# Rotary embedding of q and k: the half turn by VectorE's shuffle within 32 partitions in place of a product with a permutation matrix

## The chip, the cores and the metric

One Trainium2 chip, one of its cores. The metric is the time of one execution of the whole program on the device, in microseconds (us). A core has TensorE (matrix products into PSUM), VectorE, ScalarE (called ACT), GpSimd (called POOL) and SyncE (SP), which here only starts DMAs. The engines run their own instruction lists and meet through semaphores.

## What is computed

One inference step of a two-layer backbone for 128 context tokens and 512 latent tokens, D_MODEL 1024. Each layer: an input projection, windowed attention beside a long convolution, gates, an output projection, a layer norm, a gated MLP with a short convolution, and a second layer norm. The part that matters here is the rotary embedding of q (8 heads of 64) and k (2 heads), on the latent tokens only:

```python
def axial_rope(x):
    ...
    ang = jnp.stack([ang, ang], axis=-2).reshape(L, HEAD_DIM)
    cos = jnp.cos(ang)[None, :, None, :]
    sin = jnp.sin(ang)[None, :, None, :]
    xf = x.astype(jnp.float32)
    xa = xf.reshape(x.shape[:-1] + (2, 2, HEAD_DIM // 4))
    rot = jnp.stack([-xa[..., 1, :], xa[..., 0, :]], axis=-2).reshape(x.shape)
    return (xf * cos + rot * sin).astype(x.dtype)
...
q, k, v, z_hy, gate_a, gate_b = jnp.split(h @ lp['w_in'], SPLITS, axis=-1)
...
attn = latent_attention(axial_rope(q), axial_rope(k), v, ctx_k, ctx_v, lp['attn_sink'])
```

Within each 32 features, `rot` swaps the two halves of 16 and negates the one that comes first.

## The kernel before

**Layout.** Activations lie with features on the 128 partitions and tokens in the free dimension: q is four rows of 128 features (two heads each), k one row, v one row, each of 644 columns, of which 512 are latent (`LAT`) and 128 context (`CTX`). Swapping 16 features with their neighbours is therefore a move between partitions.

**Weights.** A weight chunk comes from HBM into one of two `w_raw` buffers (SP, line 518). ACT rounds it to its high part (`split` at line 1121, `w_hi`), VectorE subtracts that from the raw one to get the low part (`split` at line 1641, `w_lo`), and TensorE makes three products per block, high by high, low by high and high by low (`tile`, line 636 inside; `opening`, line 689, for q). Chunks 0 and 1 are q, 2 is k, 3 is v, 4 to 9 are z, two tiles each. VectorE's `split(n)` raises `w_split`, on which both TensorE and the load of a later chunk wait.

**The order by hand.** Every engine's list is written out. For the start of a layer:
- TensorE (lines 871 to 900): q, k, v; then `rotated(0)` to `rotated(3)`; z's first tile (`tile(4, 0, ...)`); `rotated(4)`; transposes of v, of the cached keys and of k's context part; z's second tile; then the scores of block 0 (`qk`), which wait for `rot_out` 5, that is for all five ropes.
- VectorE (lines 1871 to 1887): `split(2)`, `split(3)`, `split(4)`; the waits for the sine and cosine rows (`trig_in`) and, in layer 0, for earlier stores (`g_spill`); four ropes; `split(5)`; the fifth rope; `soft(0)`.
- ACT (lines 1266 to 1305): copies of q's halves out of PSUM, high parts of the chunks, copies of k and v (`qkv_out` counts them), and the copies of the transposes (`vt_out`).
- POOL (line 2208) loads `trig` once a layer, clears pad columns, and later stores the context keys and values.

`ROPE_ORDER` is k first, then q's rows 0 to 3. A rope (line 1696) waits for its product in PSUM, multiplies its row by the cosine, the product by the sine into a scratch (`tmp`, in the space of `scores`), and adds the two. The product is taken by `rotated` with the 128x128 matrix `rot`, which is loaded at the start of the program among the constants (line 1051, ACT's queue).

Of the kernel before, what the change touches and what calls it, by code (L numbers as in the profile page):

```python
# [24 lines left out]
ALU = mybir.AluOpType  # L25

P = 128
# [90 lines left out]
for _name, _n in (("b_ada", 48), ("hy_w", 36), ("hy_b", 12), ("hy_bias", 4), ("ln1_g", 8),  # L118
# [22 lines left out]
    qkv_mm=10, qkv_out=10, rot_mm=5, rot_out=5, vt_mm=2, vt_out=4,  # L141
# [93 lines left out]
def _program(nc, A):  # L235
# [11 lines left out]
    def sb(name, shape, dt=F32, where=st):  # L247
        return where.enter_context(nc.sbuf_tensor(name, shape, dt))
# [7 lines left out]
    rot = sb("rot", [P, P])  # L256
# [126 lines left out]
    ROPE_ORDER = [4, 0, 1, 2, 3]  # L383
# [143 lines left out]
    def _(pe):  # L527
# [92 lines left out]
        pe.wait_ge(sem["consts_in"], 16 * 3)  # L620
# [234 lines left out]
        for L in range(DEPTH):  # L855
# [19 lines left out]
            def rotated(at):  # L875

                r = ROPE_ORDER[at]
                pe.wait_ge(sem["qkv_out"], due("qkv_out", 5 + r))
                src = q[:, r, LAT] if r < 4 else k[:, 0, LAT]
                mm(ax[:, at % 4, :], rot[:, :], src, start=True, stop=True).then_inc(sem["rot_mm"], raised("rot_mm"))  # L880

            for at in range(4):
                rotated(at)
            pe.wait_ge(sem["w_split"], due("w_split", splits(4)))
            tile(4, 0, KD, 0, h_mov, "z_mm")
            pe.wait_ge(sem["rot_out"], due("rot_out", 1))
            rotated(4)
            pe.wait_ge(sem["qkv_out"], due("qkv_out", 10))
            pe.wait_ge(sem["rot_out"], due("rot_out", 3))
# [151 lines left out]
    def _(act):  # L1041
# [8 lines left out]
        for dst, src in ((mask_in, "mask"), (rot, "rot"), (ones, "ones")):  # L1050
            act.dma_start(dst[:, :], A[src]).then_inc(sem["consts_in"], 16)
# [445 lines left out]
    def _(dve):  # L1497
# [198 lines left out]
        def rope(r):  # L1696
# [4 lines left out]
            dve.wait_ge(sem["rot_mm"], due("rot_mm", at + 1))  # L1701
            dve.wait_ge(sem["qkv_out"], due("qkv_out", 5 + r))
            TT(row, row, trig[:, 0, :], ALU.mult).then_inc(sem["dve_order"], raised("dve_order"))
            TT(tmp, ax[:, at % 4, :], trig[:, 1, :], ALU.mult).then_inc(sem["dve_order"], raised("dve_order"))
# [150 lines left out]
        for L in range(DEPTH):  # L1855
# [15 lines left out]
            for g in range(1, 4):  # L1871
                split(g + 1)
# [3 lines left out]
            for r in ROPE_ORDER[:4]:  # L1876
                rope(r)
# [247 lines left out]
    def _(pool):  # L2125
# [61 lines left out]
        for L in range(DEPTH):  # L2187
            lane.start(L)
            if L == 0:
                pool.dma_start(par[:, 0:NPAR], A["par"][L]).then_inc(sem["params_in"], 16)  # L2190
                pool.wait_ge(sem["consts_in"], 16 * 3)
# [150 lines left out]
def _shape_constants():  # L2342
# [5 lines left out]
    r = np.zeros((P, P), np.float32)  # L2348
    for a in range(0, P, 32):
        for i in range(16):  # L2350
            r[a + 16 + i, a + i] = -1.0
            r[a + i, a + 16 + i] = 1.0
    out["rot"] = r
# [4 lines left out]
    out["trig"] = np.ascontiguousarray(np.stack([np.cos(ang), np.sin(ang)], axis=1).astype(np.float32))  # L2358
# [113 lines left out]
```

## Time and profile before

| | |
|---|---|
| median of 3 runs | 2025.42 us (2023.16 to 2025.57) |
| span of the profiled execution | 2021.7 us |
| instructions | 30180 |
| TensorE matmul busy | 1963.4 us, 97% |
| TensorE weight load busy | 1881.6 us, 93% |
| VectorE busy | 1166.7 us, 58% |
| ACT busy | 746.1 us, 37% |
| POOL busy | 199.1 us, 10% |

The profile is one execution. A row of the timeline begins with its start from the beginning of the span and its duration; in brackets stands how long the engine had been idle before it and what ended that. Matmuls overlap one another, so the sum of their durations is more than the time that they take. The chain of waits is followed back from the last instruction, at each step to what released it or to the instruction before it on its engine. Layer 0 of the network begins near 80 us, layer 1 near 1060 us; the rotation of layer 0 lies between 137 and 151 us, that of layer 1 between 1095 and 1109 us.

### The profile page before, as it was taken

How to read it: one execution, taken by the hardware profiler on the slowest of the kernel's cores; microseconds unless marked ns; L12 is line 12 of the kernel's file. 1: busy time of each engine (PE TensorE's matmuls, PEld its weight loads, DVE VectorE, ACT ScalarE, POOL GpSimd, SP SyncE). 2: the span in 40 equal slices, each digit the busy share in tenths (PEclk: the TensorE clock that was granted, in tenths of full speed). 3: DMA queues.
4: the chain of work that ended last, by engine and by line, in shares of the span. 5: the costliest groups of instructions: out<-in, count | busy, mean ns of one | idle time of the engine just before them, and what ended most of it. 6: DMA issues, size and time to landing. Idle time of an engine off the chain costs nothing.

```text
span 2021.7 us, 30180 instructions
## 1 busy us (share of the span) xinstructions
PE 1963.4 (97%) x12914; PEld 1881.6 (93%) x12914; DVE 1166.7 (58%) x1739; ACT 746.1 (37%) x1102; POOL 199.1 (10%) x218
## 2 busy tenths in 40 slices
PE   8899998999999999999999999899999999999996
PEld 3599998999999999999989999899998999999996
DVE  7735658787476777767454556852346343333335
ACT  3634445322273321333244445532227332133313
POOL 0211001100150000000121101110015000000011
PEclk9999999999999999999999999899999999999999
DMA  8522013255213345343322211322212221221121
GB/s 333 194 83 99 19 58 129 101 203 173 82 63 145 127 153 198 142 164 129 104 75 97 84 37 57 111 76 76 94 64 71 77 71 58 91 84 63 64 72 53
DMA packets 38911, 211.00 MB, mean 104 GB/s; under 512 B 4487, under 2 KB 8120, under 8 KB 20217
## 3 DMA queue, kind: packets, MB, share of 16 engines
q1 hardware_dynamic: 31480, 184.78, 25.6%
q0 software_dynamic: 4208, 17.55, 2.4%
q10 hardware_dynamic: 3088, 6.75, 0.9%
q8 instruction: 101, 1.65, 0.3%
q14 instruction: 34, 0.27, 0.0%
HBM read 198.82 MB, written 10.24 MB: 103 GB/s over the span
## 4 chain that ended last, share of the span: by engine, by line
PE 84%; DVE 9%; ACT 4%; issue 3%; POOL 0%; ACTq 0%; DMA 0%; SPq 0%; DVEq 0%; POOLq 0%
PE gemm_psum L636 51%; PE gemm_psum L666 15%; PE gemm_psum L689 3%; PE gemm_psum L649 3%; PE aux_psum L776 2%; PE gemm_psum L709 2%; PE aux_psum L757 2%; PE aux_psum L765 1%; ACT h_src_rows L1211 1%; PE gemm_psum L543 1%; PE gemm_psum L581 1%; DVE aux_psum L1820 1%; PE aux_psum L799 1%; DVE x L1824 1%; DVE w_lo L1654 0%
## 5 line engine op out<-in xcount | busy, mean ns | idle before, releaser
L636 PE MATMUL gemm_psum<-h_hi,w_hi 128*128 128x322 f32 x2144 | 497.1, 313 | 0.2
L636 PE MATMUL gemm_psum<-h_hi,w_lo 128*128 128x322 f32 x2144 | 493.4, 311 | 0.0
L636 PE MATMUL gemm_psum<-h_lo,w_hi 128*128 128x322 f32 x2144 | 491.5, 310 | 0.0
L636 PEld LDWEIGHTS gemm_psum<-h_hi,w_hi 128*128 128x128 f32 x2144 | 362.7, 189 | 4.4 <-issue 3.1
L636 PEld LDWEIGHTS gemm_psum<-h_lo,w_hi 128*128 128x128 f32 x2144 | 362.2, 189 | 0.0
L636 PEld LDWEIGHTS gemm_psum<-h_hi,w_lo 128*128 128x128 f32 x2144 | 362.0, 189 | 0.0
L1645 DVE TENSOR_TENSOR w_lo<-w_raw,w_hi 128x2048 fp32r<-128x2048 f32 (+4 forms) x124 | 237.1, 1912 | 180.1 <-ACT w_hi L1134 179.1
L1134 ACT ACTIVATE w_hi<-w_raw 128x2048 fp32r<-128x2048 f32 (+4 forms) x128 | 204.1, 1595 | 170.7 <-PE gemm_psum L666 65.6
L1552 DVE CUSTOM_DVE_ANT_0 aux_psum<-w_raw,cond_by_row 128x1024 f32<-128x1024 f32 x160 | 191.0, 1257 | 4.5 <-DMA w_raw<-in_ada_t 4.1
L1778 DVE SCALAR_TENSOR_TENSOR x<-gemm_psum,mod,x 128x128 f32<-128x128 f32 (+2 forms) x144 | 55.4, 434 | 160.6 <-PE gemm_psum L666 130.8
L666 PE MATMUL gemm_psum<-act_hi,w_lo 128*128 128x322 f32 x616 | 142.0, 312 | 0.0
L666 PE MATMUL gemm_psum<-act_lo,w_hi 128*128 128x322 f32 x616 | 141.6, 311 | 0.0
L666 PE MATMUL gemm_psum<-act_hi,w_hi 128*128 128x322 f32 x616 | 141.5, 311 | 0.0
L1680 DVE SCALAR_TENSOR_TENSOR gate_acc<-gate_rows,par,gate_acc 128x642 f32<-128x642 f32 x88 | 80.2, 912 | 76.1 <-ACT gate_acc L1219 74.6
L1851 DVE TENSOR_TENSOR gate_acc<-gate_acc,gemm_psum 128x644 f32<-128x644 f32 x40 | 33.0, 826 | 143.7 <-PE gemm_psum L636 143.7
L666 PEld LDWEIGHTS gemm_psum<-act_hi,w_hi 128*128 128x128 f32 x616 | 104.2, 189 | 0.0
L666 PEld LDWEIGHTS gemm_psum<-act_hi,w_lo 128*128 128x128 f32 x616 | 104.2, 189 | 0.0
L666 PEld LDWEIGHTS gemm_psum<-act_lo,w_hi 128*128 128x128 f32 x616 | 104.0, 189 | 0.0
L1160 ACT ACTIVATE act_hi<-gate_acc 128x644 fp32r<-128x644 f32 x44 | 32.7, 742 | 153.5 <-DVE gate_acc L1851 147.1
L1218 ACT ACTIVATE gate_rows<-gemm_psum 128x644 f32<-128x644 f32 (+1 forms) x48 | 31.8, 663 | 143.7 <-PE gemm_psum L636 139.3
L2184 POOL TENSOR_TENSOR sums<-x 128x644 f32<-128x644 f32 x4 | 6.3, 1579 | 790.5 <-DVE x L1778 790.5
L689 PE MATMUL gemm_psum<-h_hi,w_hi 128*128 128x322 f32 x224 | 72.2, 322 | 10.3 <-DVE w_lo L1654 3.4
(352 smaller groups left out, 3279.7 us busy)
## 6 DMA issues: line engine op xcount, KB each, us to landing
w_raw<-in_w_up SPq DMA_DIRECT2D x44, 1024.0 KB, 4.8
w_raw<-in_ada_t SPq DMA_DIRECT2D x42, 1024.0 KB, 4.7
w_raw<-in_w_down SPq DMA_DIRECT2D x32, 704.0 KB, 4.1
w_raw<-in_w_gate SPq DMA_DIRECT2D x16, 1024.0 KB, 4.7
w_raw<-in_w_z SPq DMA_DIRECT2D x12, 1024.0 KB, 4.7
w_raw<-in_w_out SPq DMA_DIRECT2D x8, 1024.0 KB, 4.7
g_kept<-g_rows_out POOLq DMA_DIRECT2D x10, 512.0 KB, 3.0
ada_early<-in_ada SPq DMA_DIRECT2D x4, 1024.0 KB, 19.5
```

The costliest lines, as they stand in the source:

```text
L636: last = mm(gp[:, 2 * (t % 2) + hf, 0:HALF], w[:, off + P * kk:off + P * (kk + 1)], moving(kk, lo)[:, hf * HALF:(hf + 1) * HALF], start=kk ...
L649: last = mm(gp[:, 2 * (t % 2) + hf, 0:HALF], w[:, off + P * kk:off + P * (kk + 1)], moving(kk, lo)[:, half(hf)], start=kk == 0 and n == 0, ...
L666: last = mm(gp[:, 2 * (t % 2) + hf, 0:HALF], w[:, off + P * kk:off + P * (kk + 1)], moving(kk, lo)[:, half(hf)], start=kk == 0 and n == 0, ...
L689: last = mm(banks(c, p_, hf), w[:, P * (KD * c + kk):P * (KD * c + kk + 1)], (hlo if lo else hhi)[:, kk, half(hf)], start=kk == 0 and n == ...
L709: last = mm(gp[:, 2 * ((t0 + c) % 2) + hf, 0:HALF], w[:, P * (KD * c + kk):P * (KD * c + kk + 1)], moving(kk, lo)[:, hf * HALF:(hf + 1) * ...
L757: last = mm(ax[:, n % 4, at:at + P * m], q[pr, j, tok(b)], rhs, start=True, stop=True)
L776: last = mm(ax[:, 2, HD * n:HD * (n + 1)], p_t(n)[:, P * kb:P * (kb + 1)], v[:, HD * (n % 2):HD * (n % 2 + 1)], start=kb == 0, stop=kb == ...
L1134: run(whi[s][:, 0:n], raw[st_ % 2][:, 0:n], ACT.Copy).then_inc(sem["w_hi"], raised("w_hi"))
L1552: V.tensor_tensor_reduce(out=ada_out[:, :] if first else ax[:, 2 * gr:2 * gr + 2, :].rearrange("p a b -> p (a b)"), in0=raw[n % 2][:, D_MO ...
L1645: TT(wlo[s][:, 0:n], raw[STEP[(lane.layer, "g", g)] % 2][:, 0:n], f32(whi[s][:, 0:n]), ALU.subtract).then_inc(sem["w_split"], raised("w_sp ...
L1680: STT(acc[:, 1:ROW - 1], z[:, a:a + ROW - 2], w(tap), acc[:, 1:ROW - 1], ALU.mult, ALU.add).then_inc(sem[event if tap else "dve_order"], r ...
L1778: STT(x[:, m, a:b], gp[:, 2 * (t % 2) + h, a - HALF * h:b - HALF * h], mod[:, gate + m, gr:gr + 1], x[:, m, a:b], ALU.mult, ALU.add)\
```

## The change

The matrix `rot`, its load, the five products of a layer and the semaphore `rot_mm` are removed. A rope begins with a `stream_shuffle` of its row into `tmp`, with the list `HALF_TURN`, the same for each group of 32 partitions; the multiply with the cosine waits for it, since it overwrites the row. The sign is moved into the sine rows, which are made on the host. The ropes' order is now q's rows 0 to 3, then k; on VectorE two ropes stand ahead of `split(4)` and two behind it, and k's rope stands behind `split(5)`. TensorE's waits for single ropes ahead of `rotated(4)` and the transposes are gone; the one for all five ahead of the scores stays. The waits for the constants count two loads instead of three.

```diff
-    qkv_mm=10, qkv_out=10, rot_mm=5, rot_out=5, vt_mm=2, vt_out=4,
+    qkv_mm=10, qkv_out=10, rot_out=5, vt_mm=2, vt_out=4,
...
-    rot = sb("rot", [P, P])
...
-    ROPE_ORDER = [4, 0, 1, 2, 3]
+    ROPE_ORDER = [0, 1, 2, 3, 4]
+    HALF_TURN = [(i + 16) % 32 for i in range(32)]
...
-        pe.wait_ge(sem["consts_in"], 16 * 3)
+        pe.wait_ge(sem["consts_in"], 16 * 2)
...
-            def rotated(at):
-
-                r = ROPE_ORDER[at]
-                pe.wait_ge(sem["qkv_out"], due("qkv_out", 5 + r))
-                src = q[:, r, LAT] if r < 4 else k[:, 0, LAT]
-                mm(ax[:, at % 4, :], rot[:, :], src, start=True, stop=True).then_inc(sem["rot_mm"], raised("rot_mm"))
-
-            for at in range(4):
-                rotated(at)
             pe.wait_ge(sem["w_split"], due("w_split", splits(4)))
             tile(4, 0, KD, 0, h_mov, "z_mm")
-            pe.wait_ge(sem["rot_out"], due("rot_out", 1))
-            rotated(4)
             pe.wait_ge(sem["qkv_out"], due("qkv_out", 10))
-            pe.wait_ge(sem["rot_out"], due("rot_out", 3))
...
-        for dst, src in ((mask_in, "mask"), (rot, "rot"), (ones, "ones")):
+        for dst, src in ((mask_in, "mask"), (ones, "ones")):
...
-            dve.wait_ge(sem["rot_mm"], due("rot_mm", at + 1))
             dve.wait_ge(sem["qkv_out"], due("qkv_out", 5 + r))
+            V.stream_shuffle(tmp, row, HALF_TURN).then_inc(sem["dve_order"], raised("dve_order"))
+            dve.wait_ge(sem["dve_order"], now("dve_order"))
             TT(row, row, trig[:, 0, :], ALU.mult).then_inc(sem["dve_order"], raised("dve_order"))
-            TT(tmp, ax[:, at % 4, :], trig[:, 1, :], ALU.mult).then_inc(sem["dve_order"], raised("dve_order"))
+            TT(tmp, tmp, trig[:, 1, :], ALU.mult).then_inc(sem["dve_order"], raised("dve_order"))
...
-            for g in range(1, 4):
+            for g in range(1, 3):
                 split(g + 1)
...
-            for r in ROPE_ORDER[:4]:
+            for r in ROPE_ORDER[:2]:
+                rope(r)
+            split(4)
+            for r in ROPE_ORDER[2:4]:
                 rope(r)
...
-                pool.wait_ge(sem["consts_in"], 16 * 3)
+                pool.wait_ge(sem["consts_in"], 16 * 2)
...
-    out["trig"] = np.ascontiguousarray(np.stack([np.cos(ang), np.sin(ang)], axis=1).astype(np.float32))
+    sign = np.where(np.arange(P) % 32 < 16, -1.0, 1.0)[:, None]
+    out["trig"] = np.ascontiguousarray(np.stack([np.cos(ang), sign * np.sin(ang)], axis=1).astype(np.float32))
```

## Rows read from the trace of the kernel before

**Rows 1.** The page, parts 1 and 4: busy time, and the last chain.
```profile
PE 1963.4 (97%) x12914; PEld 1881.6 (93%) x12914; DVE 1166.7 (58%) x1739; ACT 746.1 (37%) x1102; POOL 199.1 (10%) x218
...
PE 84%; DVE 9%; ACT 4%; issue 3%; POOL 0%; ACTq 0%; DMA 0%; SPq 0%; DVEq 0%; POOLq 0%
```

**Rows 2.** TensorE's waits: for whom, us in total, times, longest.
```profile
PE aux_psum L837 <- DVE y_lo L1658: 13.9, 2, 7.0
```

**Rows 3.** Windows: stretch, length; busy PE, PEld, DVE, ACT, POOL; clock, DMA share, GB/s.
```profile
137.00:158.00 21.00, 20.95 (x128) 18.11 (x126) 11.96 (x17) 5.64 (x10) 1.61 (x3) 1.00 0.38 132
```

**Rows 4.** The tile `rot`: durations in ns (min/median/max), first and last start.
```profile
L880 PE MATMUL aux_psum<-q,rot x16: 590/591/593, 138.7 to 1106.8; 128*128 128x512 f32 x16
```

**Rows 5.** Timeline of TensorE's weight loads, 137 to 142 us.
```profile
137.64 0.34 PEld L880 LDWEIGHTS aux_psum<-k,rot 128*128 128x128 f32 x2
138.22 0.19 PEld L880 LDWEIGHTS aux_psum<-q,rot 128*128 128x128 f32 x1 [0.24 <-issue]
...
140.80 0.19 PEld L636 LDWEIGHTS gemm_psum<-h_hi,w_hi 128*128 128x128 f32 x1 [0.24 <-issue]
...
141.38 0.34 PEld L636 LDWEIGHTS gemm_psum<-h_lo,w_hi 128*128 128x128 f32 x2
```

**Rows 6.** The chain of waits in order of time: start, duration, what.
```profile
137.95 3.44 PE aux_psum L880 x8
...
148.54 0.86 PE aux_psum L880 x2
...
157.31 0.47 PE aux_psum L757 x4
...
1106.54 0.86 PE aux_psum L880 x2
```

**Rows 7.** Timeline of VectorE at the start of each layer.
```profile
124.85 1.23 DVE L1645 TENSOR_TENSOR w_lo<-w_raw,w_hi 128x1024 fp32r<-128x1024 f32 x1 [5.91 <-ACT w_hi L1134]
132.85 2.29 DVE L1645 TENSOR_TENSOR w_lo<-w_raw,w_hi 128x2048 fp32r<-128x2048 f32 x1 [6.78 <-ACT w_hi L1134]
139.02 0.69 DVE L1703 TENSOR_TENSOR k<-k,trig 128x512 f32<-128x512 f32 x1 [3.88 <-PE aux_psum L880]
139.63 0.68 DVE L1704 TENSOR_TENSOR scores<-aux_psum,trig 128x512 f32<-128x512 f32 x1
140.34 0.69 DVE L1706 TENSOR_TENSOR k<-k,scores 128x512 f32<-128x512 f32 x1
140.95 0.69 DVE L1703 TENSOR_TENSOR q<-q,trig 128x512 f32<-128x512 f32 x1
...
1090.85 2.29 DVE L1645 TENSOR_TENSOR w_lo<-w_raw,w_hi 128x2048 fp32r<-128x2048 f32 x1 [6.78 <-ACT w_hi L1134]
```

**Rows 8.** VectorE by line and form (busy, mean ns), and one row of its timeline.
```profile
L1820 DVE RECIPROCAL aux_psum<-aux_psum 128x322 f32<-128x322 f32 x8 | 17.3, 2168 | 0.0
...
8.00 0.43 DVE L1515 TENSOR_SCALAR sine_turns<-h1T 128x512 f32<-128x512 f32 x1
```

**Rows 9.** Timeline of ACT, 124 to 140 us.
```profile
124.72 0.42 ACT L1239 ACTIVATE q<-gemm_psum 128x322 f32<-128x322 f32 x1
130.90 1.92 ACT L1134 ACTIVATE w_hi<-w_raw 128x2048 fp32r<-128x2048 f32 x1 [5.76 <-PE gemm_psum L636]
...
138.59 1.90 ACT L1134 ACTIVATE w_hi<-w_raw 128x2048 fp32r<-128x2048 f32 x1
```

**Rows 10.** Timeline of POOL, 95 to 108 us.
```profile
95.77 0.57 POOL L2161 DMA_DIRECT2D g_kept<-g_rows_out  x1 [0.16 <-issue]
...
107.25 0.57 POOL L2208 DMA_DIRECT2D trig<-in_trig  x1 [0.30 <-POOL h_lo L2152]
```

**Rows 11.** The start: ACT's queue, and a wait of TensorE's weight loads.
```profile
7.63 0.52 ACTq L1051 DMA_DIRECT2D rot<-in_rot  x1
...
PEld gemm_psum L543 <- DMA ada_early<-in_ada: 0.8, 1, 0.8
```

**Rows 12.** Windows behind the long convolution's wait in each layer, columns as in rows 3.
```profile
345.00:360.00 15.00, 13.75 (x89) 12.52 (x87) 14.00 (x28) 13.11 (x22) 7.85 (x6) 1.00 0.10 42
...
1300.00:1315.00 15.00, 14.51 (x96) 13.82 (x96) 13.42 (x27) 13.03 (x22) 5.68 (x6) 0.94 0.20 71
```

More of the change, by code:

```diff
@@ L2346, in _shape_constants @@
     out["ones"] = np.ones((P, P), np.float32)
[L2348 to L2353, printed above, removed]
     inv = 1.0 / (10000.0 ** (np.arange(0, 32, 2, dtype=np.float32) / np.float32(32)))
```

## The prediction

> **What bounds the kernel now.** I read the page first: TensorE is busy for 97% of the span, and the chain that ended last is 84% TensorE work [rows 1]. A microsecond taken out of TensorE's own stream is therefore worth a microsecond, unless the place where it is taken out is one where TensorE waits. The waits of TensorE come next: the longest in the whole kernel is 7.0 us, twice, once a layer, on `y_lo` of the long convolution [rows 2], and no wait there names the rotation. Then the stretch from 137 to 158 us, which holds the rotation of layer 0: TensorE is busy in 20.95 of 21.00 us, VectorE in 11.96, the granted clock is 1.00 (its 2.4 GHz level) [rows 3]. So this stretch is TensorE's, and VectorE has room in it.
>
> **Removed: the products with the permutation matrix.** A product is two passes. The tile view lists 16 passes for q's 8 products, 591 ns each [rows 4], and 4 more for k's 2. But passes overlap, so 591 ns is not the price. The price is the distance between weight loads: 137.64, 138.22, ..., and 141.38 where the z product is back at its own pace, in rows 0.43 us apart (138.22 to 140.80 holds six of them, 2.58 us) [rows 5]. The chain of waits says the same: 3.44 us for the 8 passes ahead of z's tile and 0.86 us for the two in the middle of it, 0.86 us again in layer 1 [rows 6]. That is 10 passes x 0.43 = 4.30 us a layer, 8.60 us in both, all of it on TensorE's stream with no wait inside. The neighbours (the v, z and transpose work) keep their lengths.
>
> **Added: a shuffle in each rope, on VectorE.** Before, a rope is three operations of 128x512; its rhythm is 139.02 to 140.95, 1.93 us. An operation that waits for the one in front starts 0.71 us behind it (139.63 to 140.34) [rows 7]. The change puts one more operation in front, and the multiply with the cosine, which overwrites the row, waits for it. No shuffle is in the trace. From below I bound it by a single-source operation of this size, 0.43 us; from above by the slowest kind per column that VectorE has here, the reciprocal, 2.168 us for 322 columns, so by proportion 3.45 us for 512 [rows 8]. I take the ordinary two-source operation, 0.69 us, a slot of 0.71, because it moves the same bytes: a rope is then 2.64 us.
>
> The Trainium skill (VectorE: DVE Perf Modes, "The perf-mode tier table") gives a shuffle no faster mode, about 2400 ns for 2048 columns beside 2293 for a two-source one; by that a 512-column shuffle would be an estimated 0.80 us, and the rope 2.75 us. The Trainium skill (Vector Engine (DVE) Microarchitecture Reference, 3.8 The reshape front-end and per-opcode configuration) also says that an instruction of its own loads the lane selection first, so there may be two new instructions to a rope, not one. Neither would move the sum, for the cover below is far wider; no row here shows either.
>
> **What covers the ropes, and what is late next.** Order on VectorE before: the low parts of k, v and z (`split(2)` to `split(4)`), ropes k, q0, q1, q2, `split(5)`, rope q3. After: `split(2)`, `split(3)`, ropes q0, q1, `split(4)`, ropes q2, q3, `split(5)`, rope k. Before, VectorE is idle for 6.78 us in front of `split(4)` and for 3.88 us in front of the first rope [rows 7]. What moves in front of `split(4)` must be ready by 126.08, the end of `split(3)` (124.85 + 1.23): the last of q's four rows is copied at 124.72 + 0.42 [rows 9], the sine and cosine rows are asked for at 107.25, and the last spill that the ropes of layer 0 wait for is issued at 95.77 [rows 10]. So ropes q0 and q1 run from 126.08 to 131.36. `split(4)` needs ACT's high part, done at 130.90 + 1.92 = 132.82 [rows 9], so it starts at 132.85 and ends at 135.14 as before, with 1.5 us to spare. TensorE wants it at 137.64 [rows 5], 2.5 us later still. The same places in layer 1 stand at 1090.85, again behind 6.78 us of idle time [rows 7].
>
> Behind it, q2 and q3 run to 140.42; ACT's high part for `split(5)` is done at 138.59 + 1.90 = 140.49 [rows 9], hung on the v product's end and so unmoved; `split(5)` ends at about 142.8 and rope k at 145.5. TensorE reaches the scores of block 0, which wait for all ropes, at 157.31 before [rows 6] and at 153.01 after. Rope k, now the last, has 7.5 us of cover. The cost of the added VectorE work (5 x 0.71 = 3.6 us a layer) is therefore nothing. If the first cover is gone, each further microsecond of a rope delays `split(4)` by two; the place and point are priced below. Nobody is queued behind the moved `split(4)` but the load of the next weights, whose issue is tied to it: at the old time. `split(5)` finishes at 142.8 instead of 149.03 (139.02 + 4 x 1.93 + 2.29), so the load behind it goes out 6 us sooner; it lands ahead of need either way, so I cost it at nothing. The wait of the transposes on the ropes (`rot_out` 3) goes too; it was over before they were reached, and v's row, which they do need, was copied long before.
>
> **Everything behind.** ACT's copies of v, GpSimd's stores and combines, and the scores all hang on TensorE's transposes and tiles, which move together by 4.30 us, so they keep their places to one another. In the long convolution TensorE's 7.0 us wait hangs on a VectorE chain which itself starts from a product of TensorE, so it moves along.
>
> **At the start** the load of `rot` leaves ACT's queue: 0.52 us of issuing ahead of the first sine [rows 11]. Gain at most 0.55 us. I take 0: TensorE soon waits 0.8 us for the landing of the first modulation weights [rows 11], more than the half microsecond. From the other side, the loads behind it start that much sooner and share the engines with those weights, so a loss of as much is possible.
>
> **Clock.** Behind the 7.0 us waits the granted clock sinks below its upper level; 15 us on it is 1.00 in layer 0 but 0.94 in layer 1 [rows 12], that is 15 x 0.06 = 0.9 us that one layer pays and the other does not, at otherwise equal work. A shift of 4.3 us can flip this in either layer: 0 taken, -0.9 to +1.8 as bounds.
>
> **The sum** is made against the profiled execution, 2021.7 us of span, 3.7 us below the median 2025.42 of the runs shown (lowest 2023.16): 2021.7 - 8.60 = 2013.1 us of span, and by the same 3.7 us a median of 2016.8 us, 0.42% less.
>
> **Rivals.**
> - *A slow shuffle, the side on which it loses.* With a rope of r us, `split(4)` is late by 2r - 9.27 (from 126.08 to 137.64, less 2.29 for the split), and from its end the scores by 3r + 2.29 - 15.06 more (three ropes and `split(5)` against z's tiles and the transposes: 157.31 - 141.39 - 0.86 = 15.06 by [rows 6]). Together 5r - 22.04; it eats the 4.30 us at r = 5.27, a shuffle slot of 3.34 us, and loses 0.2% only from a slot of 3.74 us. At the reciprocal's pace, slot 3.47 and r 5.40, each layer loses 0.66 us: 2026.7 us. For it: that no row shows a shuffle, and that its lanes cross. Against: a reciprocal computes and a shuffle only moves, as the operation of 0.43 us does, and the rope's own three take 0.69 us [rows 7, 8]. Chance 0.04, with half of that beyond 0.2% slower.
> - *The gain stops at the long convolution.* If the VectorE chain behind the 7.0 us wait had its foot off TensorE, the wait would grow to 11.3 us and the time stay at 2025.4; in one layer only, 2021.1. Against: the chain of waits runs through TensorE's transposes and z tiles up to that stage. Chance 0.06 for both layers, 0.06 for one.
> - *The passes were hidden.* Were part of the 4.30 us hidden by something that z's product waits for anyway, the time would lie between. Against: the weight loads follow without a stop at both ends [rows 5]. With a give-back of 2 to 4 us by the clock or the loads it makes 2019 to 2021: chance 0.04.
>
> **How the numbers follow.** The forecast, a gain of 8.6 us with its small terms, has 0.80. Its own range: -0.55 and -0.9 below, +0.5 and +1.8 above, and below that the runs of before, which reach 2.3 us under their median: 2013.8 to 2019.5. To keep no more than 2 in 10 outside, the upper end takes in part of the one-layer case: 2013.5 to 2020.5. About 0.2% (4.05 us) is what a measurement of this kernel can tell from no change. Faster by more than that, under 2021.4, are the forecast, the one-layer case and the partly hidden passes: 0.90. Within it: the case of both layers and half the slow shuffle, 0.08. Slower: 0.02.
>
> **What would show it.** In the profile after: no passes of the rotation; the v product followed at once by z's first tile, near 137.6; five shuffles a layer of some 0.7 us; two ropes ended ahead of `split(4)`, which still starts by 133; no wait of TensorE that names the low part of z or rope k; the scores of block 0 near 153; the wait on `y_lo` still 7 us. A shuffle slot over 1.45 us would shift `split(4)`, one over 2.70 us would stop TensorE. A longer `y_lo` wait, or a clock in the convolution stage below that of before, would make the number wrong.

## The result, and the profile after

| | before | after |
|---|---|---|
| median | 2025.22 us (2023.16 to 2025.57, 4 runs) | 2034.55 us (2031.60 to 2035.25, 4 runs) |
| span of the profiled execution | 2021.7 us | 2033.4 us |

After divided by before is 1.0045, 95% interval 1.0032 to 1.0058: slower, where 2016.8 us and faster were predicted. (The two profiled executions are 11.7 us apart, the medians 9.3 us: before's profile is near the fastest of its executions, after's is the slowest.) The instruction counts moved by what the diff says: 20 TensorE passes fewer and 20 VectorE instructions more than in [rows 1] (ten shuffles, each with a small instruction ahead of it). Page of the profile after, parts 1, 3 and 4; q10 is ACT's DMA queue:

```profile
PE 1957.1 (96%) x12894; PEld 1879.5 (92%) x12894; DVE 1172.7 (58%) x1759; ACT 745.6 (37%) x1102; POOL 199.2 (10%) x218
...
q10 hardware_dynamic: 2944, 6.69, 0.9%
...
PE 82%; DVE 9%; ACT 4%; issue 2%; ACTq 1%; DMA 1%; POOL 0%; SPq 0%; DVEq 0%
```

What is new in it is "ACTq 1%": 1% of a chain of 2033 us, where [rows 1] has 0%, spent in issuing a DMA. TensorE's waits in the profile after (for whom, us in total, times, longest) say where:

```profile
PE aux_psum L553 <- ACT h1T L1081: 19.1, 1, 19.1
PE aux_psum L837 <- DVE y_lo L1646: 13.9, 2, 7.0
```

The second line is [rows 2], unmoved. The first is the first use of ACT's sines, at the very start of the program; before, the same wait was 2.7 us long:

```profile
PE aux_psum L553 <- ACT h1T L1093: 2.7, 1, 2.7
```

ACT's timeline after, and under it the same stretch of before:

```profile
8.26 0.62 ACTq L1040 DMA_DIRECT2D x<-in_x_prompt  x1
8.91 17.57 ACTq L1041 DMA_DIRECT2D x<-in_x_sample  x1
26.51 1.28 ACT L1043 ACT_TABLE_LOAD   x1 [26.51 <-issue]
```

```profile
8.73 0.62 ACTq L1052 DMA_DIRECT2D x<-in_x_prompt  x1
9.38 0.76 ACTq L1053 DMA_DIRECT2D x<-in_x_sample  x1
10.17 1.28 ACT L1055 ACT_TABLE_LOAD   x1 [10.17 <-issue]
```

The issue of the last load of the start, x_sample, takes 17.57 us instead of 0.76. Nobody wants x before 78 us (in before), but ACT's list stands still behind it, and its first sine comes 16.3 us later. So the loss is at the start, far from the rotation. The rotation itself did what was predicted. The chain of waits after, in both layers (start, duration, what; L636 is the product of v and then of z, L757 the scores of block 0):

```profile
140.48 21.44 PE gemm_psum L636 x144
...
169.83 0.47 PE aux_psum L757 x4
...
1097.09 21.45 PE gemm_psum L636 x144
...
1126.44 0.47 PE aux_psum L757 x4
```

v's product begins at 140.48 where before it began at 123.66 (16.82 us later), but the scores begin at 169.83 against 157.31 [rows 6], only 12.52 us later: 4.30 us won between them, as predicted. In layer 1 it is 1097.09 against 1081.66 (15.43 later) and 1126.44 against 1115.31 (11.13 later): 4.30 us again. Between the two rotations this execution lost 2.91 us (12.52 to 15.43), and 0.57 us behind the second (11.13 to the 11.7 of the whole span). 2.0 of the 2.9 us went ahead of layer 0's output product, which begins at 520.58 against 506.06. VectorE's timeline after, which answers to [rows 7]:

```profile
142.82 0.01 DVE L1690 LOAD_MASK_SELECT scores<-q  x1
142.82 0.73 DVE L1690 STREAM_SHUFFLE scores<-q 128x512 f32<-128x512 f32 x1
143.58 0.69 DVE L1692 TENSOR_TENSOR q<-q,trig 128x512 f32<-128x512 f32 x1
...
145.53 0.01 DVE L1690 LOAD_MASK_SELECT scores<-q  x1
...
149.68 2.29 DVE L1633 TENSOR_TENSOR w_lo<-w_raw,w_hi 128x2048 fp32r<-128x2048 f32 x1 [1.35 <-ACT w_hi L1122]
```

A shuffle takes 0.73 us, its slot is 0.76 us (142.82 to 143.58), a rope 2.71 us (to 145.53). `split(4)` still waits 1.35 us for ACT: the two ropes ahead of it are covered.

### The profile page after: what moved, and what is told of

Read it like the earlier page. It is cut to its first block, busy times and chain, and to the rows that moved or that the text cites. A ratio compares the mean times of both kernels' runs of the same rounds, so it can differ in the third digit from the quotient of the medians.

```text
span 2033.4 us, 30146 instructions
## 1 busy us (share of the span) xinstructions
PE 1957.1 (96%) x12894; PEld 1879.5 (92%) x12894; DVE 1172.7 (58%) x1759; ACT 745.6 (37%) x1102; POOL 199.2 (10%) x218
## 3 DMA queue, kind: packets, MB, share of 16 engines
q10 hardware_dynamic: 2944, 6.69, 0.9%
## 4 chain that ended last, share of the span: by engine, by line
PE 82%; DVE 9%; ACT 4%; issue 2%; ACTq 1%; DMA 1%; POOL 0%; SPq 0%; DVEq 0%
PE gemm_psum L636 49%; PE gemm_psum L666 15%; PE gemm_psum L689 3%; PE gemm_psum L649 3%; PE aux_psum L776 2%; PE gemm_psum L709 2%; PE aux_psum L757 2%; PE aux_psum L799 1%; PE aux_psum L765 1%; ACT h_src_rows L1199 1%; PE gemm_psum L581 1%; ACTq L1041 1%; DVE aux_psum L1809 1%; DVE w_lo L1642 1%; PE gemm_psum L543 1%
## 5 line engine op out<-in xcount | busy, mean ns | idle before, releaser
L636 PE MATMUL gemm_psum<-h_hi,w_hi 128*128 128x322 f32 x2144 | 496.6, 313 | 1.8 <-DVE w_lo L1642 1.2
L636 PE MATMUL gemm_psum<-h_hi,w_lo 128*128 128x322 f32 x2144 | 493.5, 311 | 0.0
L636 PE MATMUL gemm_psum<-h_lo,w_hi 128*128 128x322 f32 x2144 | 491.5, 310 | 0.0
L636 PEld LDWEIGHTS gemm_psum<-h_hi,w_hi 128*128 128x128 f32 x2144 | 362.5, 189 | 5.7 <-issue 2.8
L636 PEld LDWEIGHTS gemm_psum<-h_lo,w_hi 128*128 128x128 f32 x2144 | 362.2, 189 | 0.0
L636 PEld LDWEIGHTS gemm_psum<-h_hi,w_lo 128*128 128x128 f32 x2144 | 362.0, 189 | 0.0
L689 PE MATMUL gemm_psum<-h_hi,w_hi 128*128 128x322 f32 x224 | 72.3, 323 | 10.7 <-POOL h_lo L2144 3.7
## 6 DMA issues: line engine op xcount, KB each, us to landing
ada_early<-in_ada SPq DMA_DIRECT2D x4, 1024.0 KB, 19.5
```

The costliest lines, as they stand in the source:

```text
L636: last = mm(gp[:, 2 * (t % 2) + hf, 0:HALF], w[:, off + P * kk:off + P * (kk + 1)], moving(kk, lo)[:, hf * HALF:(hf + 1) * HALF], start=kk ...
L689: last = mm(banks(c, p_, hf), w[:, P * (KD * c + kk):P * (KD * c + kk + 1)], (hlo if lo else hhi)[:, kk, half(hf)], start=kk == 0 and n == ...
```

## The experiments

### Is it the missing load?

The theory with which I began: ACT's queue had room for x_sample only because of what stood ahead of it. The rivals were the shuffle and everything else in the diff. Two runs, one that puts a load back and one that makes only that part of the change.

**e1_load_back**: after, with a load of 64 KB in the place of the one of `rot`, into a tile that nobody reads.

```diff
-        for dst, src in ((mask_in, "mask"), (ones, "ones")):
+        for dst, src in ((mask_in, "mask"), (spare, "ones"), (ones, "ones")):
```

> The changed kernel with a 64 KB load put back on ACT's queue where the matrix was loaded, into a tile that nobody reads; its source is the matrix of ones, so the matrix of the permutation stays away from the program. Theory A (the start is lost because ACT's queue has one load less, everything else of the prediction holds): the issue of x_sample falls from 17.57 us back to about 0.8 us, the median is that of before less 8.6 us, 2016.6 us. Rival B (the loss comes from the addresses or the set of tensors, not from the queue): 2034 us as the changed kernel. Rival C (the shuffles cost elsewhere too): between, over 2020 us.

Measured: 2018.25 us median (2017.36 to 2019.15, 5 runs) against 2025.41 for before, ratio 0.9964 (0.9950 to 0.9978), span 2016.4. The stop is gone, by one unread load (ACT's timeline):

```profile
9.39 0.77 ACTq L1042 DMA_DIRECT2D x<-in_x_sample  x1
```

**e2_before_rot_on_pool**: before, with only the load of `rot` moved from ACT's queue to POOL's.

```diff
-        for dst, src in ((mask_in, "mask"), (rot, "rot"), (ones, "ones")):
+        for dst, src in ((mask_in, "mask"), (ones, "ones")):
...
+                pool.dma_start(rot[:, :], A["rot"]).then_inc(sem["rot_in"], 16)
```

> The kernel before, products and all, with one part of the change alone: the matrix is no longer loaded on ACT's queue but on POOL's. Theory A: ACT's issue of x_sample stalls for some 17 us and the time is 2025 + 17 = 2042 us, with no shuffle in the program. Rival B (tensors or addresses): no stall, 2025 us.

Measured: 2042.42 us, span 2040.2, with all the products of the rotation in it. ACT's timeline:

```profile
8.86 17.62 ACTq L1054 DMA_DIRECT2D x<-in_x_sample  x1
```

The stop is there without a shuffle and without any other part of the change, and costs what it costs in after. So the load that left ACT's queue is the cause; the two runs show it from both sides. They also settle rival B: e2 keeps the tensor `rot` and its tile where they were, and still stops.

### What in the load matters?

Its 64 KB, its moment (half a microsecond), its number in the list, or its packets? A packet here is one piece of a load on one DMA engine. The page's part 3 gives the measure: ACT's queue has 3088 packets before and 2944 after, that is 193 and 184 for each of the 16 DMA engines. The load of `rot` is the difference, 9 packets on each; a load of x is 65. Ahead of x_sample stand 128 on each engine before (seven loads of 9 and x_prompt) and 119 after. The Trainium skill (DMA: Bandwidth & Descriptors, "Queues, rings and completion order") says that each queue has a ring of its own on each DMA engine, with its own tail pointer, which is why I count by engine; it gives no size at which an issue stops.

**e3_one_packet**: after, with a load of 16 partitions in the place of `rot` (2 packets on each engine where `rot` had 9, so 121 ahead; "a ninth" in the expectation is wrong).

```diff
+        act.dma_start(spare[0:16, :], A["ones"][0:16, :]).then_inc(sem["consts_in"], 16)
```

> As the run that puts a load back, but of 16 partitions of 512 bytes, 8 KB: nearly the same time of issuing, a ninth of the packets. If what counts is when x_sample is issued (8.91 us in the changed kernel, 9.38 us before) or how many loads stand ahead of it, no stall: 2016.6 us. If what counts is how many packets stand ahead of it in the queue, the stall is there: 2034 us.

**e4_wait**: after, ACT issues x_sample only when two sines' arguments are there, 2 us later.

```diff
+        act.wait_ge(sem["mlp_arg"], 2)
         act.dma_start(x[:, :, LAT], A["x_sample"]).then_inc(sem["x_in"], 16)
```

> The changed kernel; ACT waits for VectorE's second piece of sine arguments (near 10.9 us) before it issues x_sample. If the moment of the issue decides, the stall is gone and the time 2017 to 2019 us; if the packets ahead of it decide, the issue still ends near 26.5 us and the time is 2034 us.

**f2_swapped**: after, x_sample ahead of x_prompt.

> The changed kernel with x_sample issued ahead of x_prompt. Theory D (the large load of 2 MB is what can't be taken): x_sample, now with fewer packets ahead, stalls. Theory E: x_sample goes from 54 to 119 and is issued in 0.8 us, x_prompt goes from 119 to 184 and stalls to about 26.5 us; time 2034 us.

**f4_in_halves**: after, x_sample in two loads of four rows each.

```diff
+        act.dma_start(x[:, 0:4, LAT], A["x_sample"][:, 0:4]).then_inc(sem["x_in"], 16)
+        act.dma_start(x[:, 4:8, LAT], A["x_sample"][:, 4:8]).then_inc(sem["x_in"], 16)
```

> The changed kernel with x_sample loaded in two halves of 33 packets per DMA engine. Theory E: the first half (119 to 152) passes 128 and stalls; if the stall lasts until what is behind 128 has room, its issue ends earlier than 26.5 us (a shorter piece behind the mark), and the second half then takes the rest of the wait; time 2030 to 2034 us. Theory D (one load must not be larger than some size): no stall, 2017 us.

Measured, all four with the loss still there: 2034.94, 2034.70, 2036.04 and 2035.03 us. ACT's timelines, e3, e4, f2 and f4 in this order:

```profile
9.40 18.09 ACTq L1043 DMA_DIRECT2D x<-in_x_sample  x1
```

```profile
11.08 15.32 ACTq L1042 DMA_DIRECT2D x<-in_x_sample  x1
```

```profile
8.28 0.62 ACTq L1040 DMA_DIRECT2D x<-in_x_sample  x1
8.93 17.56 ACTq L1041 DMA_DIRECT2D x<-in_x_prompt  x1
```

```profile
8.80 17.61 ACTq L1041 DMA_DIRECT2D x<-in_x_sample  x1
26.44 0.53 ACTq L1042 DMA_DIRECT2D x<-in_x_sample  x1
```

e3: a load in the old place, but of 2 packets in place of 9, does not help. x_sample is asked for at 9.40, as before the change, and behind as many loads, so neither the count of loads nor half a microsecond decides. e4: 2.2 us later, the stop ends at the same 26.40 us. f2: the other load stops when it stands second, so it is the place and not the tensor. f4: half a load stops as long as a whole one (not for a shorter time, as theory E had it), and the half behind it does not stop at all. The load that stops has 119 (or 121) packets ahead of it, whatever it is.

### The rule: first theory wrong

By then I held that ACT stops on the load whose packets pass the 128th, since before the change x_prompt ended exactly at 128. Two runs on either side of it.

**g2_one_packet_less**: as e1, but the load put back has 112 partitions (8 packets on each engine; x_sample has 127 ahead).

> The kernel after with the load put back as in the run that removed the stall, but of 112 partitions instead of 128: one packet less on each DMA engine of ACT's queue (8 instead of 9), so x_prompt ends at the 127th and x_sample goes from the 128th to the 192nd. Theory 'position': x_sample passes the 128th, so it stops for 15 to 18 us and the span is 2031 to 2036 us. Rival 'any load in that place of about this size is enough': no stall, 2015 to 2019 us of span.

**g1_two_loads**: after with two loads of 9 packets more (x_prompt has 72 ahead and passes 128, x_sample has 137). The second one is 112 columns wide, 56 KB; f1, the same with two full tiles, has no time, since SBUF was 64 bytes a partition short for it.

> The kernel after with two 64 KB loads ahead of the two loads of x (one of them in the place of the load of rot, the other behind that of ones), so that ACT's queue holds 72 packets of each DMA engine ahead of x_prompt instead of 63 (before) or 54 (after). Theory 'position': ACT stops on the load whose packets pass the 128th of each engine of its queue; now x_prompt does that (72 to 137), so x_prompt's issue takes 15 to 18 us and x_sample's under 1 us, and the span is 2031 to 2036 us. Rival 'enough ahead': the stall comes only when too little stands ahead of x_sample; then neither stops, and the span is 2015 to 2019 us. If x_sample stops again and x_prompt doesn't, both are wrong.

Measured: g2 2032.89 us, as the theory has it; g1 2039.69 us, but not as it has it. ACT's timelines, g2 and then g1:

```profile
9.32 18.18 ACTq L1043 DMA_DIRECT2D x<-in_x_sample  x1
```

```profile
9.19 0.62 ACTq L1043 DMA_DIRECT2D x<-in_x_prompt  x1
9.84 17.79 ACTq L1044 DMA_DIRECT2D x<-in_x_sample  x1
```

In g1 x_prompt passes the 128th and takes 0.62 us; x_sample stops with 137 ahead. So passing 128 is not it. What is left is that it goes by how much stands ahead, with 128 as an exception. One packet less (g2) or nine more (g1) than before the change, and the stop is there.

**g4_other_128**: after, nothing added, mask and ones in two pieces each and x_prompt in eight: 128 ahead of x_sample, in 16 loads.

```diff
+            for a in (0, 64):
+                act.dma_start(dst[a:a + 64, :], A[src][a:a + 64, :]).then_inc(sem["consts_in"], 16)
+        for j in range(8):
+            act.dma_start(x[:, j, CTX], A["x_prompt"][:, j]).then_inc(sem["x_in"], 16)
```

> The kernel after with the loads ahead of x_sample cut up, nothing added: mask and ones in two pieces of 64 partitions each, x_prompt in eight (one for each row of 128 features). A piece costs one more packet on each DMA engine, so 36 + 4 x 5 + 8 x 9 = 128 packets of each engine stand ahead of x_sample, as before the change, but in 16 loads instead of 8. Theory 'exactly 128': x_sample's issue takes under 1 us (the start is later by the 9 more issues, 0.5 us each, so the span is 2018 to 2023 us). Rival 'it is not the count: the stall comes in any list other than the one of before (seven constants and one load of x)': x_sample or one of the pieces ahead of it takes 10 to 18 us, and the span is over 2028 us.

**g5_fewer_ahead**: after, ones behind the loads of x: 110 ahead of x_sample, 175 ahead of ones.

> The kernel after with the load of ones moved behind the two loads of x: 45 packets of each DMA engine ahead of x_prompt and 110 ahead of x_sample (after: 54 and 119). Theory A: whoever is issued with more than some number between 72 and 110 ahead stops, unless that number is 128; then x_sample's issue takes 14 to 18 us, ending near 26 us, and the span is over 2030 us. Theory B: the bound lies between 110 and 119 (as it would if only a load passing 175 to 184 in total stopped); then x_sample takes under 1 us and ones, with 175 ahead, stops in its place. In either case the time itself says little, since ones lands behind x.

Measured: 2038.11 and 2035.77 us. ACT's timelines, g4 (three narrow stretches show pieces alone) and g5:

```profile
11.83 4.53 ACTq L1042 DMA_DIRECT2D x<-in_x_prompt  x1
11.83 8.66 ACTq L1042 DMA_DIRECT2D x<-in_x_prompt  x2
...
20.51 6.08 ACTq L1042 DMA_DIRECT2D x<-in_x_prompt  x2
26.62 0.61 ACTq L1043 DMA_DIRECT2D x<-in_x_sample  x1
```

```profile
8.42 15.27 ACTq L1040 DMA_DIRECT2D x<-in_x_sample  x1
23.73 6.27 ACTq L1041 DMA_DIRECT2D ones<-in_ones  x1
```

In g4 the first four pieces (56, 65, 74 and 83 ahead) go out at 0.45 to 0.63 us each; the fifth, with 92 ahead, ends at 16.36, the sixth (101) at 20.49, the seventh (110) at 23.54, the eighth (119) at 26.59. And with 110 ahead g5's x_sample, a load seven times as large, ends at 23.69: theory A of its expectation, though ones, with 175 ahead, stops as well. Beside each other, with what is left of the packets ahead at that moment (counted as below):

| packets ahead on each engine | runs | the issue ends at (us) | left on each engine |
|---|---|---|---|
| 54 to 83 | all that ask for one at the start | at once | |
| 92, 101 | g4 | 16.36, 20.49 | 72, 75 |
| 110 | g4, g5 | 23.54, 23.69 | 76 |
| 119 | after, e2, e4, f2, f4, g4, g6 | 26.40 to 26.59 | 78 to 79 |
| 121, 127, 137 | e3, g2, g1 | 27.49, 27.50, 27.63 | 77, 83, 92 |
| 128 | before, e1, e5, h1 | at once (0.76 to 0.78 us) | 122 |
| 128 | g4 | at once (asked at 26.62) | 88 |
| 152 | f4 | at once (asked at 26.44) | 111 |
| 175 | g5 | 30.00 | 111 |

How far the queue is by then can be counted. The DMA view of the profile after from 0 to 26.5 us (packets, MB, share of the engines' time):

```profile
q10 hardware_dynamic: 661, 3.89, 35.4%
```

661 / 16 = 41 of the 119 are through, so 78 stand in the queue when the issue goes on; over the rows from 92 to 121 it is 72 to 79. It fits that g4's piece with 83 ahead was asked for with some 73 left and did not stop, and the next one, with 92 ahead, was asked for with some 81 left (181 packets through) and did. That explains why the stop is so long: it lasts until some 40 packets of each engine, most of them of 4 to 12 KB, have gone through engines that carry the modulation weights at the same time.

What is shown is that the issue of a load stops its engine until the queue has drained some way, and that up to 121 ahead it goes on with 72 to 79 left. One bound for all rows is not shown: with 127, 137 and 175 ahead the stop ended with 83, 92 and 111 left, f4's second half went at once with 111 left and g4's x_sample with 88. The exception of 128 rests on four kernels with one and the same list (seven loads of 9 packets and one of 65); g4 could not decide between "exactly 128" and "that list", since its own 128 was reached only when the queue had drained. Both stay open.

### Can the loads go elsewhere?

**f3_x_later**: after, both loads of x issued by ACT behind the first rows of the filter spectrum (34 us); no load put back.

> The changed kernel with both loads of x issued by ACT behind its first two copies of the filter spectra (near 33 us), when its queue has drained, and no load put back. The stall is gone: the gain of 8.6 us stands alone, 2016.6 us, or up to 1 us less since ACT issues 2 us less ahead of its first sine (TensorE waits there for the first modulation weights anyway). If x then lands late for layer 0 (needed near 79 us) or ACT's issues push the filter work, 2018 to 2020 us.

**g6_x_in_gap**: the same at 24 us, ahead of a stretch in which ACT is idle.

```diff
         pre_split(1)
+        act.dma_start(x[:, :, CTX], A["x_prompt"]).then_inc(sem["x_in"], 16)
+        act.dma_start(x[:, :, LAT], A["x_sample"]).then_inc(sem["x_in"], 16)
```

> The kernel after with both loads of x issued by ACT behind the high part of the second filter block (near 25 us, in a stretch where ACT is idle for 3.48 us) instead of ahead of the first sine; no load put back. Theory: the stall needs over 72 packets of each engine outstanding, and by then the constants are nearly through, so none of the two stops; the issues (1.4 us) fall into idle time, the first sine comes 1.4 to 2.0 us earlier than in the run with the load put back, and TensorE's wait of 2.7 us for it shrinks. Span 2013.5 to 2016.5 us, median 2015 to 2018.5 us. Rival: the earlier sine only brings TensorE to a wait for the modulation weights, which land when they land: no gain over the run with the load put back (span 2016 to 2017). If x_sample stalls at the new place, the span is over 2018 us.

**g3_x_on_pool**: after, both issued by POOL.

> The kernel after with both loads of x issued by POOL (behind its load of par), which waits until 31 us for the constants anyway; no load put back. ACT's queue then holds 54 packets of each DMA engine at the start and never passes 128 there. Theory 'position': ACT does not stop; its first sine comes 1.4 us earlier than in the run with the load put back (8.8 instead of 10.2 us), and the two loads are POOL's, where the second may stop behind 128 of its own (65 + 65 and par's 9) at no cost if it ends before 31 us. Span 2014 to 2018 us, median 2016 to 2020 us. Rival 'the shuffle or the lost load slows the start in another way': a wait of TensorE of over 10 us ahead of 31 us stays, and the span is over 2030 us. Contrary possibility: POOL stops for longer than until 31 us and delays the mask and the first low parts; then the span lies between 2018 and 2032 us.

**e5_load_back_again**: e1's kernel beside g6.

> The same kernel as the run with the load put back, for comparison with the one ahead of it on the same chip: median 2016.5 to 2019.5 us, span 2015.5 to 2017.5 us, x_sample's issue 0.8 us.

| | median (runs) | before | ratio (95%) | span |
|---|---|---|---|---|
| f3_x_later | 2018.64 (6) | 2025.09 | 0.9967 (0.9955 to 0.9979) | 2018.1 |
| g6_x_in_gap | 2018.84 (6) | 2024.96 | 0.9970 (0.9958 to 0.9981) | 2017.9 |
| g3_x_on_pool | 2025.45 (10) | 2025.30 | 1.0001 (0.9991 to 1.0010) | 2025.4 |
| e5_load_back_again | 2016.88 (5) | 2024.96 | 0.9961 (0.9947 to 0.9974) | 2014.2 |

Without a stop the first sine does come earlier (the table load ahead of it at 8.05 us in f3, 8.29 in g6, 10.19 in e1), and it is worth nothing, as g6's rival had it: TensorE then waits for the weights. f3 and g6 both missed the gain that was expected of them (medians of 2016.6 and at most 2018.5 us, without the late x that f3's other range stands for); the intervals of their ratios overlap e5's. Their traces even begin layer 0's v product later than before's 123.66: at 126.34 and 124.81. It is not a wait but the granted clock. Windows of f3 (two) and, beside them, e1 (columns as in rows 3); g6's clock is 0.79 in the second one:

```profile
24.00:30.00 6.00, 5.82 (x10) 1.13 (x11) 5.27 (x7) 2.25 (x4) 0.00 (x0) 0.72 1.03 418
64.00:72.00 8.00, 6.03 (x21) 4.53 (x20) 7.83 (x13) 3.23 (x6) 0.53 (x1) 0.83 0.67 280
```

```profile
64.00:72.00 8.00, 6.03 (x23) 3.54 (x22) 7.86 (x13) 3.83 (x7) 0.82 (x2) 1.00 0.54 223
```

In f3 the first eight products behind the wait for the weights take 5.29 us where e5's take 3.60, and twelve products near 68 us take 4.58 us in f3 and g6 where before's take 3.05. Whether the earlier sine brings this about is not shown: h1 below, whose start is e1's, has it near 68 us too.

TensorE's waits of g6 and of g3:

```profile
PE gemm_psum L543 <- DMA ada_early<-in_ada: 1.5, 2, 1.3
```

```profile
PE gemm_psum L543 <- DMA ada_early<-in_ada: 6.3, 1, 6.3
```

In g3 that wait is 6.3 us: POOL's queue puts the packets of x beside the modulation weights from the start, where on ACT's queue they stood behind the constants. The weights then land 24.9 us behind their issue (median of four) against 19.5 before. VectorE's longest wait for the products behind them is 10.7 us, 2.8 before, and the whole gain is gone. The range of 2014 to 2018 us of span missed; the time lies in that of the contrary possibility, but not for its reason, since POOL's issues took 0.92 and 0.89 us. g6 still had a short stop: x_sample took 1.55 us and ended at 26.44, the time for 119 ahead.

### Where did the rest of the gain go?

e1's span was 5.3 us under before instead of 8.6. Its gate stage in layer 0 had given back 1.8 us, where ACT waited for the gate weights:

```profile
433.79 1.92 ACT L1123 ACTIVATE w_hi<-w_raw 128x2048 fp32r<-128x2048 f32 x1 [2.84 <-DMA w_raw<-in_w_gate]
```

The load was issued at 426.58, so it took 7.2 us to here, against 4.75 in before (430.90 to 435.65); TensorE waited 1.6 us for the gates. I took two packets of program code ahead of it on one DMA engine for the cause and tested that.

**h1_list_padded**: e1 with 27 waits that are already over on TensorE in each layer, where the products stood.

```diff
+            for _ in range(27):
+                pe.wait_ge(sem["qkv_out"], due("qkv_out", 5))
```

> The kernel of the run with the load put back (no stall) and, in each layer, 27 waits on TensorE that are already over, in the place where the products with rot stood, so that TensorE's instruction list is about as long as before. What it tests: in that run the gate weights of layer 0 took 7.2 us to land instead of 4.7 us, because one of the 16 DMA engines first carried two packets of program code (0.51 and 1.12 us); TensorE waited 1.6 us for the gates and 1.8 of the 4.3 us were given back there. Theory 'code': the moment of those packets goes by the place in the instruction lists; with the list as long as before they come at the old distance from the gate weights' load, the landing is back at about 4.7 us, the wait of 1.6 us goes, and the span is 1 to 2 us under the 2016.4 us of that run, less what 27 waits cost TensorE (0 to 1.5 us a layer). Rival 'order of loads': the late landing comes from loads that are issued 4.3 us earlier against others that are not; then the padding leaves the 7.2 us and the 1.6 us as they are and the span is 2016 to 2019 us.

Measured: 2017.75 us median (4 runs), ratio 0.9962 (0.9947 to 0.9977), span 2016.7, not 1 to 2 us under e1's 2016.4. The gate weights were on time (4.7 us, from 429.76 to 434.42) and the wait was gone, as the theory had it. But e5, e1's own kernel with nothing changed, also had them in 5.1 us (426.16 to 431.27), and the wait was gone there too:

```profile
431.27 1.92 ACT L1123 ACTIVATE w_hi<-w_raw 128x2048 fp32r<-128x2048 f32 x1 [0.74 <-DMA w_raw<-in_w_gate]
```

So it comes and goes between executions of one kernel, and h1 proves nothing for the code packets; what delays that one load stays open. The padding itself costs nothing where it stands: v's and z's products take 21.44 us with it and without. h1 also began q's products 3.2 us later than e1 (98.11 against 94.92), ahead of the padding. That is the granted clock again: 0.82 from 64 to 72 us, where the window of e1 above has 1.00 and TensorE has waited 1.97 us ahead of the same products in both, and 0.81 from 80 to 98 us against e1's 0.91. By 8 x 0.18 + 18 x 0.10 it is an estimated 3.2 us. Window of h1:

```profile
64.00:72.00 8.00, 6.03 (x20) 3.89 (x19) 7.83 (x14) 2.93 (x6) 0.53 (x1) 0.82 0.51 210
```

With e5, a profile without that delay, the prediction's sum can be laid beside the trace. The chain of waits, e5, then before, at the same places (products of v and z of layer 0; output product; MLP; products of v and z of layer 1; scores of block 0):

```profile
123.21 21.44 PE gemm_psum L637 x144
...
152.56 0.47 PE aux_psum L758 x4
...
501.31 14.28 PE gemm_psum L710 x96
...
602.48 122.09 PE gemm_psum L637 x816
...
1078.49 21.44 PE gemm_psum L637 x144
...
1107.84 0.47 PE aux_psum L758 x4
```

```profile
123.66 14.29 PE gemm_psum L636 x96
...
506.06 14.28 PE gemm_psum L709 x96
...
606.76 121.76 PE gemm_psum L636 x816
...
1081.66 14.30 PE gemm_psum L636 x96
...
1115.31 0.47 PE aux_psum L757 x4
```

e5 is ahead of before by 0.45, 4.75 (152.56 against the 157.31 of [rows 6]), 4.75, 4.28, 3.17 and 7.47 us. So each layer's rotation gives 4.30 us; the first 4.30 reach the output product whole, 1.58 are lost on the way to layer 1, in the norms and the MLP, and the second 4.30 reach the end: 7.5 us of span, 8.1 us in the medians. These are two single executions, and e5's five lie 2.4 us apart, so it is not shown that the 1.58 us belong to the change.

## Why the prediction was wrong

- **What failed is one term, "At the start".** I had counted that the load's 0.52 us of issuing goes, asked who would gain or lose half a microsecond, and set 0, with bounds of 0.55 us on one side and 0.5 on the other. Measured: 16.8 us lost (v's product of layer 0 at 140.48 instead of 123.66). With the 8.6 us won and the 3.5 us lost elsewhere in that execution it makes the 11.7 us between the profiles. The half microsecond was rightly judged worthless, since f3 and g6 issue two loads fewer there and gain nothing; what was missing is that the load was part of what stood ahead of x_sample, and that the issue of a load can itself stop its engine. The row was there to be suspicious of (x_sample's issue at 9.38, with eight loads in front of it), but no row of before shows a stop, so its size could not have been read from that trace. It could have been a rival: a moved load changes the state of the queue for all the loads behind it. My rivals were all about the rotation, and none covered this.
- **Removed products: right.** 10 passes at 0.43 us, 4.30 us a layer, measured 4.30 in both layers of after and of e5.
- **The shuffle: right.** Taken 0.69 us and a slot of 0.71; it is 0.73 and 0.76, a rope 2.71 us against 2.64. The estimate of 0.80 us by the Trainium skill (VectorE: DVE Perf Modes, "The perf-mode tier table") was 10% high. What the prediction took from the Trainium skill (Vector Engine (DVE) Microarchitecture Reference, 3.8 The reshape front-end and per-opcode configuration) holds: a `LOAD_MASK_SELECT` stands ahead of each shuffle, for 0.01 us.
- **The cover: right.** `split(4)` waits 1.35 us for ACT behind its two ropes, predicted 1.5; TensorE waits for neither it nor rope k, and the scores of block 0 begin at 152.56 in e5 where 153.01 was forecast.
- **Everything behind: right as far as the output product, then 1.58 us short** in e5; in after 2.9 us short, 2.0 of them ahead of the output product. The shifts were taken to pass through unchanged, and by these single executions they do so only within 1 to 3 us. The `y_lo` waits kept their 13.9 us in all [rows 2]. The rival of a gain that stops at the long convolution is out.
- **Clock.** Within the bounds, but the reading of [rows 12] was wrong: its windows do not answer to each other. TensorE's wait on `y_lo` ends at 338.43 in layer 0 and at 1296.43 in layer 1, so the first window begins 6.6 us behind it and the second 3.6. Laid as far behind as the second, layer 0's window has 0.98 against 0.94, 0.6 us instead of the 0.9 of the prediction. At the same distance (the wait ends at 1307.58 in after and 1288.95 in e5) layer 1 has 0.97 in after (1311.15 to 1326.15) and 1.00 in e5. Windows of before (layer 0) and e5 (layer 1), columns as in rows 3:

```profile
342.00:357.00 15.00, 14.12 (x96) 13.32 (x96) 13.34 (x27) 13.07 (x22) 5.73 (x6) 0.98 0.20 71
```

```profile
1292.50:1307.50 15.00, 13.54 (x95) 12.74 (x94) 13.40 (x27) 13.06 (x22) 5.68 (x6) 1.00 0.18 70
```

- **The range.** Its terms, 0.55, 0.9 and 2.3 us below and 0.5 and 1.8 above 2016.8, give 2013.1 to 2019.1, not 2013.8 to 2019.5. It matters little beside a miss of 18 us.
- **The sum.** 2016.8 us was forecast for the rotation alone; with the place of the load kept, the same kernel measures 2018.25 and 2016.88 us (e1, e5). It beats both kernels, by an unread load of 64 KB whose only work is to keep the list ahead of x_sample as it was; with one packet less on each engine (g2) the stop is back. The later place (f3, 2018.64 us) costs no such load.

## What to carry to other kernels

Removing a DMA is not free by itself: write down what stands ahead of each later load on the same queue, and look in the new profile at the durations of the DMA-issuing rows first, since a stop there shows as the length of such a row: TensorE's list of waits named ACT's sine here, and no DMA. Put a load that nobody wants for a long time behind the work of its issuing engine, or on an engine with nothing behind it, but not so that its packets run beside those that the start waits for. And when an expected gain turns into a loss that is larger, take the one moved load back alone before looking at the arithmetic.

## What the runs showed of the hardware

- ACT's issue of a DMA takes 0.4 to 0.9 us, but 1.55 to 18.2 us when some 80 or more packets are still ahead on each DMA engine of its queue. For 92 to 121 ahead it goes on when 72 to 79 are left, whatever the size of the load (33 and 65 packets end within 0.1 us of each other, 9 and 65 within 0.15). Two loads went at once with 88 and 111 left, 128 and 152 ahead (g4, f4).
- With 128 ahead, in the one list that was tried at the start, the same load goes at once; with 127 it takes 18.18 us and with 137 it takes 17.79.
- `STREAM_SHUFFLE` of 128x512 float32 takes 0.73 to 0.75 us, the load of its selection 0.01 us.
- The same 1 MB load in the same kernel was ready after 5.1 us in one execution and 7.2 us in another (e5, e1), worth 1.6 us of TensorE's time.
- The granted clock in the same stretch of two kernels with the same start differed between executions: 1.00 in e1 and 0.82 in h1 from 64 to 72 us, behind a wait of TensorE of 1.97 us in both.
